# VectorE alone splits the first weights and adds the squares, the column sums go among the first token tile's products, and attention starts two sub-tiles later

## The reference, cut to what matters

```python
xn   = rms_norm(x) * g_pre
proj = xn @ w_in                      # columns: qa ka va za | qm km vm om zm | ig fg
att  = window_attention(qa, ka, va)   # window 128, sinks, ALiBi;   a_out = att * silu(za)
h    = mlstm(qm, km, vm, ig, logsigmoid(fg))   # chunks of 128, running maximum, states C, n, m
m_out = sigmoid(om) * rms(h) * silu(zm)
y    = x + rms_norm(concat(a_out, m_out) @ w_out) * g_post
```

## Time and profile before

| | us |
|---|---|
| median of 3 runs | 569.39 (569.07 to 569.61) |
| profiled execution | 567.94 |
| its span, first to last instruction | 566.1 |
| PE busy | 550.7 (97%) |
| DVE busy | 281.8 (50%) |
| ACT busy | 210.0 (37%) |
| POOL busy | 156.7 (28%) |
| granted TensorE clock, mean | 0.991 of full speed |

### The profile page before, as it was taken

How to read it: one execution, slowest core, us unless ns; L and a number is a source line. 1 busy time by engine, 2 the same in 40 slices (tenths; PEclk the granted TensorE clock), 3 DMA queues, 4 the chain that set the end, 5 groups by cost and what they waited for, 6 DMA issues and landing times.

```text
span 566.1 us, 10430 instructions
## 1 busy us (share of the span) xinstructions
PE 550.7 (97%) x4325; PEld 507.5 (90%) x4325; DVE 281.8 (50%) x497; ACT 210.0 (37%) x538; POOL 156.7 (28%) x146
## 2 busy tenths in 40 slices
PE   8979999999799999999999999999999999999996
PEld 8979999999788989899898989899999998888874
DVE  4984655774155656530376767425333327042223
ACT  7722322341344454542565645244322234021011
POOL 2732533402132434341113131246322220011001
PEclk9989999999899999999999999999999999999998
DMA  8820000272122212113233321321123215043321
GB/s 292 301 74 2 1 1 1 62 267 75 38 75 64 86 63 63 40 38 90 69 94 112 94 75 40 93 75 38 38 75 100 87 38 186 0 164 133 108 97 56
DMA packets 36262, 48.20 MB, mean 85 GB/s; under 512 B 4128, under 2 KB 28128, under 8 KB 36200
## 3 DMA queue, kind: packets, MB, share of 16 engines
q1 hardware_dynamic: 27224, 43.15, 24.0%
q10 hardware_dynamic: 8992, 4.40, 2.8%
HBM read 39.96 MB, written 8.56 MB: 86 GB/s over the span
## 4 chain that ended last, share of the span: by engine, by line
PE 85%; DVE 6%; DMA 3%; issue 2%; ACT 2%; SPq 1%; POOL 1%; DVEq 0%; POOLq 0%; ACTq 0%
PE ps L590 45%; PE ps L496 8%; PE ps L497 8%; PE ps L498 8%; DVE x_hl L1145 2%; PE ps L638 2%; PE ps L664 2%; DMA w_raw<-in_w_in_tiles 2%; PE ps L738 2%; PE ps L750 1%; PE ps L714 1%; PE ps L740 1%; DMA xT_raw<-in_x_T 1%; DVE wt_lo L1159 1%; PE ps L774 1%
## 5 line engine op out<-in xcount | busy, mean ns | idle before, releaser
L590 PE MATMUL ps<-x_hl,w_hi 128*128 128x368 f32 (+1 forms) x1104 | 277.4, 332 | 0.7 <-POOL w_lo L343 0.7
L590 PEld LDWEIGHTS ps<-x_hl,w_hi 128*128 128x128 f32 x1104 | 193.9, 188 | 7.5 <-issue 5.9
L590 PE MATMUL ps<-x_hl,w_lo 128*128 128x368 f32 (+1 forms) x552 | 181.7, 329 | 0.0
L590 PEld LDWEIGHTS ps<-x_hl,w_lo 128*128 128x128 f32 x552 | 104.0, 188 | 0.1
L993 ACT ACTIVATE prob<-prob,nmx 128x160 f32<-128x160 f32 x64 | 26.6, 417 | 47.0 <-DVE sd L1298 47.0
L343 POOL TENSOR_TENSOR w_lo<-w_raw,w_hi 128x1024 fp32r<-128x1024 f32 x12 | 29.5, 2462 | 49.5 <-ACT w_hi L903 49.4
L1643 POOL TENSOR_TENSOR qmT<-qmT,sg 128x368 f32<-128x368 f32 (+1 forms) x24 | 25.0, 1042 | 57.8 <-DVE sg L1488 36.4
L496 PE MATMUL ps<-wt_hi,x_hl 128*128 128x324 f32 x128 | 40.5, 316 | 0.0
L498 PE MATMUL ps<-wt_hi,x_hl 128*128 128x324 f32 x128 | 40.4, 316 | 0.0
L497 PE MATMUL ps<-wt_lo,x_hl 128*128 128x324 f32 x128 | 40.3, 315 | 0.0
L1593 POOL TENSOR_TENSOR prob<-prob,rden 128x640 f32<-128x640 f32 x16 | 20.1, 1254 | 60.2 <-DVE rden L1304 60.2
(11 more groups left out here) (244 smaller groups left out, 953.3 us busy)
## 6 DMA issues: line engine op xcount, KB each, us to landing
w_raw<-in_w_in_tiles SPq DMA_DIRECT2D x23, 512.0 KB, 3.8
w_raw<-in_w_out_tiles SPq DMA_DIRECT2D x8, 512.0 KB, 3.6
x_res<-in_x_prompt SPq DMA_DIRECT2D x8, 512.0 KB, 4.2
xT_raw<-in_x_T SPq DMA_DIRECT2D x7, 544.0 KB, 8.0
out_y_prompt<-y_out SPq DMA_DIRECT2D x7, 512.0 KB, 2.9
wt_raw<-in_w_tok SPq DMA_DIRECT2D x4, 648.0 KB, 12.1
Cs<-in_state_C SPq DMA_DIRECT2D x16, 128.0 KB, 2.3
Gt<-r_rows ACTq DMA_DIRECT2D x8, 256.0 KB, 3.5
```

What stands on the lines that cost most here:

```text
L590: last = mm(ps[:, 6 + sub % 2, 0:w], wt, xt, start=(at_ == 0), stop=(at_ == 23))
```

## The change

The first two weight tiles' lo moves from POOL to DVE (`first_lo`), and all seven additions of squares are on DVE, one slice behind, into one accumulator, with two more buffers for squares (`sq_b`, `sq_c`). PE's column sums are no longer a block ahead of the first token tile: they stand one by one behind its products with the hi weights; then the products with the lo weights, the spread, and half 1. Attention starts at sub-tile 18 in place of 16; the gate rows are transposed behind sub-tile 15. The loads of tiles 4 to 7 move ahead in SP's queue, the two copies of the window caches from DRAM to DRAM behind them.

```diff
-S_P2 = S_KM + 1
+S_P2 = S_KM + 3
@@ SP
         load_w(2)
         load_w(3)
+        load_w(4)
         wait(sp, "tok_done", NTILE)
...
         sp.dma_start(bias_s[:], i["bias_sample"]).then_inc(s("bias_ld"), 16)
+        load_w(5)
         sp.wait_ge(s("vrow_st"), 16)
...
-        for name, cache in (("win_k_sample", "cache_win_k"), ("win_v_sample", "cache_win_v")):
-            sp.dma_start(o[name]..., i[cache]...).then_inc(s("out"), 16)
-        load_w(4)
-        load_w(5)
+        load_w(6)
         wait(sp, "rows_done", 1)
...
+        load_w(7)
+        for name, cache in (("win_k_sample", "cache_win_k"), ("win_v_sample", "cache_win_v")):
+            sp.dma_start(o[name]..., i[cache]...).then_inc(s("out"), 16)
@@ PE
-        def square_sums():
-            wait(pe, "acc_done", KT // 2 + 1)
+        def square_sum(t):
+            if t == 0:
+                wait(pe, "acc_done", KT - 1)
...
         def first_token_tile():
-            for q in range(2):
-                if q == 1:
-                    wait(pe, "rstd_act", 1)
-                for kk in range(KT):
-                    if q == 0 and kk == 5:
-                        spread_rstd()
-                    if q == 0:
-                        wait(pe, "wt_split_d", kk // 2 + 1)
-                    last = token_products(0, kk, q)
+            def product(q, kk, pas):
...
+                wait(pe, "wt_split_d" if pas == 2 else "wt_hi_a", kk // 2 + 1)
...
+            for kk in range(KT):
+                product(0, kk, 0)
+                product(0, kk, 1)
+                square_sum(kk)
+            square_sum(NC)
+            for kk in range(KT):
+                product(0, kk, 2)
+            spread_rstd()
+            wait(pe, "rstd_act", 1)
+            for pas in range(3):
+                for kk in range(KT):
+                    last = product(1, kk, pas)
...
-        project(24 * 8)
+        project(24 * (S_KM + 1 - S_F - 1))
         wait(pe, "rows_done", 1)
...
-        project(24 * (S_P2 - S_KM))
+        project(24 * (S_P2 - S_KM - 1))
@@ ACT
                 if sub == S_KM:
+                    wait(act, "rows_done", 1)
+                if sub == S_P2:
                     act.wait_ge(s("m_out"), 16)
+                    act.wait_ge(s("rrow_st"), 32)
                     wait(act, "cols_ps", 1)
@@ DVE
+        def first_lo(kk):
+            wk = slice(kk * P, (kk + 1) * P)
+            wait(dve, "w0_hi", kk + 1)
+            TT(w_lo[:, :, wk], w_raw[:, :, wk], w_hi[:, :, wk].bitcast(F32), ALU.subtract).then_inc(s("w0_lo"), 1)
...
         for kk in range(KT):
             first_hi(kk)
+            first_lo(kk)
+            if kk >= 2:
+                add_squares(kk - 1)
             x_lo(kk)
-            if kk % 2 == 1:
-                add_squares(kk)
-        add_squares(KT)
+        add_squares(KT - 1)
```

More of the change, by code:

```diff
@@ L175, in build @@
     wt_raw = sb("wt_raw", [P, KT, TOK_W], F32, Dr + 4 * KT * TOK_W)
-    acc_2 = sb("acc_2", [P, T], F32, GI + 18688)
+    sq_b = sb("sq_b", [P, T], F32, GI + 18688)
+    sq_c = sb("sq_c", [P, T], F32, Dr + 8 * KT * TOK_W)
     x_sc = sb("x_sc", [P, 2, KT, P], F32, Dr + 8 * KT * TOK_W)
@@ L180, in build @@
     gates = sb("gates", [P, NTILE, 2 * PQ], F32, GI + 16384)
-    row = [sb(f"row{n}", [MH, T], F32, Dr + n * 4 * T) for n in range(6)]
+    row = [sb(f"row{n}", [MH, T], F32, Dr + n * 4 * T if n else Fr + 8 * T) for n in range(6)]
     ib, fb, ra, rb, rc, rd = row
@@ L303, in square_at @@
     def square_at(kk):
-        return acc[:] if kk == 0 else acc_2[:] if kk == 2 else sq[:, kk // 2 if kk < 4 else kk % 2, :]
+        return [acc[:], sq[:, 0, :], sq[:, 1, :], sq_b[:], sq_c[:], sq[:, 0, :], sq[:, 1, :], sq_b[:]][kk]
     def sub_of(sub):
@@ L397, in _ @@
         sp.dma_start(va_w[:, 1, :, :], v_band(1)).then_inc(s("vw_ld1"), 16)
-        for name, cache in (("win_k_sample", "cache_win_k"), ("win_v_sample", "cache_win_v")):
-            sp.dma_start(o[name][0, :, 0:WIN - DEC_T].rearrange("b w k d -> b (w k d)"),
-                         i[cache][0, :, DEC_T:WIN].rearrange("b w k d -> b (w k d)")).then_inc(s("out"), 16)
-        load_w(4)
-        load_w(5)
+        load_w(6)
         wait(sp, "rows_done", 1)
@@ L406, in _ @@
         sp.dma_start(gl_rows, r_gl[:, T_P:T]).then_inc(s("rrow_st"), 16)
+        load_w(7)
+        for name, cache in (("win_k_sample", "cache_win_k"), ("win_v_sample", "cache_win_v")):
+            sp.dma_start(o[name][0, :, 0:WIN - DEC_T].rearrange("b w k d -> b (w k d)"),
+                         i[cache][0, :, DEC_T:WIN].rearrange("b w k d -> b (w k d)")).then_inc(s("out"), 16)
         def load_c(r):
@@ L421, in store_c @@
                 sp.dma_start(o["C_sample"][0, bs, h].rearrange("b d v -> d b v"), Cs[:, bs, 0:MD]).then_inc(s(f"c_st{r % 2}"), 16)
-        for n in range(6, len(SEQ)):
+        for n in range(8, len(SEQ)):
             kind, j = SEQ[n]
@@ L521, in first_tiles @@
                                 last.then_inc(s("sub_done"), 1)
-        def square_sums():
-            wait(pe, "acc_done", KT // 2 + 1)
[L525 to L529, removed]
+        def square_sum(t):
+            if t == 0:
+                wait(pe, "acc_done", KT - 1)
+                wait(pe, "ones_ready", 1)
+            off, n = x_cols(t)
+            last = mm(ps[0:n, 7, TOK_H + 4 + t:TOK_H + 5 + t], acc[:, off:off + n], ones[:, 0:1], start=True, stop=True)
+            if t == NTILE - 1:
+                last.then_inc(s("ss_cols"), 1)
         def spread_rstd():
@@ L560, in first_token_tile @@
         def first_token_tile():
-            for q in range(2):
-                if q == 1:
-                    wait(pe, "rstd_act", 1)
-                for kk in range(KT):
-                    if q == 0 and kk == 5:
-                        spread_rstd()
-                    if q == 0:
-                        wait(pe, "wt_split_d", kk // 2 + 1)
-                    last = token_products(0, kk, q)
+            def product(q, kk, pas):
+                xt, wt = x_hl[:, 1 if pas == 1 else 0, kk * T:kk * T + P], wt_lo if pas == 2 else wt_hi
+                wait(pe, "wt_split_d" if pas == 2 else "wt_hi_a", kk // 2 + 1)
+                return mm(ps[:, TOK_BANK[0] + q, 0:TOK_H], xt, wt[:, kk, q * TOK_H:(q + 1) * TOK_H],
+                          start=(kk == 0 and pas == 0), stop=(kk == KT - 1 and pas == 2), skip_group_check=True)
+            for kk in range(KT):
[8 more added lines that the diff above has]
+            for pas in range(3):
+                for kk in range(KT):
+                    last = product(1, kk, pas)
             last.then_inc(s("tok_done"), 1)
@@ L600, in _ @@
         first_tiles()
-        square_sums()
         first_token_tile()
@@ L864, in square @@
         def square(kk):
-            wait(act, "acc_done", {4: 1, 5: 2, 7: 3}.get(kk, 0))
-            wait(act, "acc2_done", 1 if kk == 6 else 0)
+            wait(act, "acc_done", kk - 4)
             A_(square_at(kk), xT_raw[:, kk, :], ACT.Square).then_inc(s("sq_ready"), 1)
@@ L1146, in x_lo @@
                 op0=ALU.mult, op1=ALU.subtract).then_inc(s("xl_ready"), 1)
+        def first_lo(kk):
+            wk = slice(kk * P, (kk + 1) * P)
+            wait(dve, "w0_hi", kk + 1)
+            TT(w_lo[:, :, wk], w_raw[:, :, wk], w_hi[:, :, wk].bitcast(F32), ALU.subtract).then_inc(s("w0_lo"), 1)
         def add_squares(kk):
[L1149 to L1154, removed]
+            wait(dve, "acc_done", kk - 1)
+            wait(dve, "sq_ready", kk + 1)
+            TT(acc[:], acc[:], square_at(kk), ALU.add).then_inc(s("acc_done"), 1)
         def wt_lo_part(g):
@@ L1215, in _ @@
             first_hi(kk)
+            first_lo(kk)
+            if kk >= 2:
+                add_squares(kk - 1)
             x_lo(kk)
-            if kk % 2 == 1:
-                add_squares(kk)
-        add_squares(KT)
-        for g in range(4):
-            wt_lo_part(g)
+        add_squares(KT - 1)
+        wt_lo_part(0)
+        wt_lo_part(1)
+        wt_lo_part(2)
+        wt_lo_part(3)
         mean_squares()
@@ L1236, in _ @@
         wait(dve, "rows_ps", 1)
+        wait(dve, "x_scaled", NTILE)
         for dst, bias, q in ((ib, bgi, 0), (fb, bgf, PQ)):
```

## The result

| | before | after |
|---|---|---|
| median, in one set of runs | 569.23 (567.91 to 569.61, 4 runs) | 565.05 (564.52 to 565.95, 4 runs) |
| ratio, 95% interval | | 0.9926 (0.9913 to 0.9939) |
| profiled execution, its span | 567.94, 566.1 | 565.95, 564.1 |

The change makes the kernel faster by 4.2 us; 7.9 were forecast, and 565.05 lies 0.25 us above the upper end of the range. The two profiled executions differ by 2.0 us only: the one of after is the slowest of its four (granted clock 0.989 of full speed; the other three have 0.991 to 0.994). So what is read from the traces has to add up to 2.0, not to 4.2.

A forecast was written before the change was run, and what follows sets the result against it. PE was taken as the bound, busy 550.7 of 566.1 us, so only its idle and half-clock time could be won. 3.4 + 0.7 + 4.8 - 1.0 = 7.9 gave a 561.5 us median, range 559.5 to 564.8.

The forecast's parts named there:

- First stage: Start through first token tile: DVE finishes its slices sooner, PE follows, and the tile ends 3.4 us earlier.
- Clock behind it: Behind the spread in the first token tile: 24 products partly at half clock, 1.0 us lost, bounds 0 and 2.2.
- Loads: Weight tile 4, issued far ahead of its use, no longer makes PE wait: 0.7 us saved.
- Attention: Ahead of the first scores: two sub-tiles cover ACT's chain, removing a 3.2 us gap and 1.6 of half clock, 4.8 saved.
- The border at sub-tile 39: End of attention: two free sub-tiles go, but tile 14 keeps a 2 us margin, so the cost is 0.
- the rival that ends slower: At sub-tile 39, tile 14 lands late under a full queue and holds ACT and PE: 570.7 us or more, chance 0.04.
- No clock loss: At the start, products among the sums keep PE at 2.4 GHz: gain 8.9, 560.5 us, chance 0.27.
- attention still waits: Something other than ACT's chain holds the first scores: gain stated as 8.0 - 4.8 = 3.1, 566.3 us, chance 0.05.
- the start gives nothing: The clock falls among the column sums, cancelling the start's gain: total gain 0.7 + 4.8, 563.9 us, chance 0.17.

The follow-up runs named there:

- sub-tile 17 and products: The changed kernel with attention starting at sub-tile 17 instead of 18 and 12 and 6 unread matmuls in PE's two start waits: 559.60 us.
- The run with before's start: The changed kernel with its first-stage edits undone, keeping the moved loads and attention from sub-tile 18: 568.16 us.
- sub-tile 16: The changed kernel with attention from sub-tile 16 and rows transposed behind sub-tile 14, as in before; only start and loads remain changed: 565.85 us.
- The last pair: The changed kernel with attention from 17 and 12 and 6 unread matmuls in PE's start waits, without and with POOL's split held back in attention: 559.60 and 558.47 us.
- The early load: The changed kernel with ACT's first gate-row load issued right behind the last attention output, ahead of the state loads and tiles 14 and 15: 562.63 us.
- sub-tile 17: The changed kernel with attention starting at sub-tile 17 instead of 18, leaving one free sub-tile behind the copy of the keys: 561.52 us.

## Why the prediction was right in direction and too low in time

The sum, on the axis of the profiled executions: 7.9 forecast, 2.0 in the traces.

- **First stage, 3.4: right in its mechanism.** Durations, cycle (3.13) and spread (38.95 against 39.2) came out within 0.3 us. With the clock held up (sub-tile 17 and products) x_sc stands 3.75 ahead of before, 3.4 being the term.
- **Clock behind it, counted at 1.0: mis-sized.** 3.4 less the 1.0 that arrived is 2.4, and against the run whose clock held it is 2.7 (47.52 and 44.78), both beyond the 2.2 taken as the upper bound. That bound took 0.25 us per product from 8 counted in 2 us, where the starts in before stand 0.27 apart, and it left out the spread, which took 1.68 in place of 1.28. The row from 38 to 40 us was read as a slow stretch that cost nothing. The run with before's start has the slow level behind the same sequence too, only later, where it costs; and the change put real work into that place. The Trainium skill (TensorE: Matmul & The Clock Gate, Part 1) has the slow level as the default, released by activity; the trace agrees here, 0.50 from 40 to 46 us behind the waits and 1.00 from 48 us on. The prediction named that rule with 2.2 for it, and chose the middle.
- **Loads, 0.7: right.** The shift grows from 1.0 to 1.9 us between the first token tile and sub-tile 12.
- **Attention, 4.8: right for the gap and its slow stretch, but 1.2 came back inside.** Cover was counted for ACT's chain at the front; that attention's own steps have so little slack was not weighed. Of the 1.5 that are missing here, 1.2 are the two waits; 0.3 stays open. The long maxima were in before too (1.12 at every third step), and PE had no wait there: with the gap put back (sub-tile 16) both waits are absent, and the last maximum stands 5.4 us behind its scores again. The last pair shows the price of the split's place, 1.1 us. The maximum reads two tiles in SBUF while POOL reads others; the Trainium skill (SBUF — State Buffer, Summary: rules for kernel authors) says that the later of two such instructions blocks fully until the first has finished, and the trace agrees, to 0.01 us.
- **The border at sub-tile 39, counted at 0: the step that failed.** The place was the right one, and the rival that ends slower stood there, but the transfer was the wrong one. Tile 14, on which the step worked out a margin of 2 us, came in time: its split at 271.60 waited for no DMA. What was late was a load that the step didn't list, the gate rows on ACT's queue, because it now was issued among the others. It cost 1.9 us of waiting and, with the half clock, 3.2 in all (5.2 to 2.0). The early load took 2.4 off the median, sub-tile 17 avoided the wait.

The four deviations, from these terms: -1.4 (2.4 forecast, 1.0 came), +0.2, -1.5 (4.8 forecast, 3.3 came, from 1.9 to 5.2), -3.2: 7.9 - 5.9 = 2.0. "No clock loss" and "attention still waits" didn't occur (the gain of the second is 7.9 - 4.8 = 3.1; the 8.0 in its sum is a slip); "the start gives nothing" gave about the right size for a wrong reason, since start and loads are most of what the change gains. That the medians differ by 4.2 and the traces by 2.0 is the scatter of single executions: those of after span 1.4 us, those of before 1.7, and the pair profiled took the slowest of the one and nearly the fastest of the other.

On the medians the account shifts. There the start gave 3.0, more than the 3.4 - 1.0 = 2.4 counted for it, and the two sub-tiles 0.8 of 4.8. So the start falls short of its terms in the pair of traces only (its slow stretch costs time all the same: holding the clock took 561.52 to 559.60), while attention and the border fall short in both. A before that itself loses time to the clock at its start, as the run with before's start does, would explain the difference; how many of before's executions do so isn't shown.

## What to carry to other kernels

When work moves towards a border, list every transfer that is issued there, on all queues, and ask for each what is in flight ahead of it; a margin for the largest one says nothing about the small one behind it. A slow stretch of TensorE that costs nothing stands in front of a wait: before moving anything there, ask whether real work will stand behind it, and fill the waits with idle matmuls if so. And a gap that is closed on the busiest engine takes away slack from every chain that fed it: look for steps of those chains that are longer than their like (0.16 and 1.12 us for one instruction) before counting the whole gap as gained.

## What the runs showed of the hardware that was not expected

- Loads on different queues are not apart: 256 KB on ACT's queue landed in 7.6 us instead of 3.2 to 3.8, when 1.0 MB had been issued on SP's queue within the 2.3 us before and 0.5 MB followed 0.18 us behind; issued 2 us ahead of the same transfers it landed in at most 3.6.
- The same instructions at the start had a granted clock of 0.50 from 38 to 40 us in before, and of 0.60 and 0.54 from 42 to 46 us in the run with before's start; what lies behind it came 1.9 us later in the second, 0.4 of which stood there before the spread.
- A matmul of 128 columns took 0.12 us at full clock (12 in 1.45). With 12 and 6 of them in the two waits of the start the granted clock stayed at 1.00 there, and the work behind came 2.7 us earlier than in after (x_sc at 44.78 and 47.52) although no matmul of the computation was taken away.
